# Input norm of block 0 on ScalarE, meta transposes between block 1's; expert counts and gate transposes from expert 0 to expert 2

## The reference

```
h = layer_norm(concat(meta, x))                 # 272 rows x 1024, "input norm"
mix = hybrid_mixer(h)                           # h @ w_in (1024 x 3096), conv, two chunked scans, @ w_out
h = layer_norm(alpha*h + mix)
ff = moe_ffn(h)                                 # 32 experts, top 4 per token, clamped SwiGLU
out = layer_norm(alpha*h + ff)[:, 16:]
# per expert: hid = swiglu(xb @ w_gate + b_gate, xb @ w_up + b_up); yb = hid @ w_down + b_down
# each of w_gate, w_up, w_down is 1024 x 1024 in float32, 4 MB; 32 experts make 403 MB
```

## Time and profile before

| what | value |
|---|---|
| median of 3 runs | 1059.69 us (1058.49 to 1059.8) |
| the profiled execution's own time | 1057.99 us |
| its span in the trace | 1056.2 us |
| PE, PEld busy | 1019.8 us (97%), 448.6 us (42%) |
| DVE, ACT, POOL busy | 228.7 us, 143.8 us, 30.6 us |
| read from memory | 424.59 MB, 403 GB/s over the span |

### The profile page before, as it was taken

The page is one execution under the profiler, slowest core; times in us unless marked ns, Lnnn a source line. Parts: engine busy times, 40 slices in busy tenths (PEclk is TensorE's granted clock), DMA queues, the critical chain, the costliest instruction groups (busy, mean ns, idle before and its releaser), DMA issues.

```text
span 1056.2 us, 12142 instructions
## 1 busy us (share of the span) xinstructions
PE 1019.8 (97%) x5116; PEld 448.6 (42%) x5116; DVE 228.7 (22%) x495; ACT 143.8 (14%) x348; POOL 30.6 (3%) x50
## 2 busy tenths in 40 slices
PE   8999999999999999999999999999999999999997
PEld 7888764333333333332333333333333333233332
DVE  5453652111111111111111112211111111111112
ACT  3312331111111111101110011111111111011102
POOL 1230100000000000000000000000000000000000
PEclk9999999999999999999999999999999999999999
DMA  9894889999999999999999999999999999999995
GB/s 314 274 412 191 267 314 357 432 426 436 431 429 430 433 432 431 431 434 432 431 431 434 431 429 430 431 433 430 431 428 434 432 432 429 434 426 426 428 419 238
DMA packets 40587, 426.21 MB, mean 404 GB/s; under 512 B 6986, under 2 KB 19411, under 8 KB 24036
## 3 DMA queue, kind: packets, MB, share of 16 engines
q1 hardware_dynamic: 38516, 424.12, 95.9%
q10 hardware_dynamic: 2032, 1.53, 0.6%
HBM read 424.59 MB, written 1.05 MB: 403 GB/s over the span
## 4 chain that ended last, share of the span: by engine, by line
PE 69%; DMA 29%; ACT 1%; DVE 0%; issue 0%; SPq 0%; POOL 0%; DVEq 0%; POOLq 0%; ACTq 0%
PE bank L1215 29%; DMA ring<-in_moe_w_up 18%; PE bank L1266 15%; DMA ring<-in_moe_w_gate 11%; PE bank L1195 4%; PE bank L1187 4%; PE bank L871 3%; PE bank L886 2%; PE bank L1061 2%; PE bank L1049 1%; PE bank L1003 1%; PE bank L1257 1%; PE bank L1135 1%; PE bank L964 1%; PE bank L1069 1%; PE bank L1235 1%
## 5 line engine op out<-in xcount | busy, mean ns | idle before, releaser
L1215 PE MATMUL bank<-ring,arena 128*64 128x512 f32 x1980 | 444.5, 601 | 24.5 <-DMA ring<-in_moe_w_up 20.7
L1215 PEld LDWEIGHTS bank<-ring,arena 128*64 128x64 f32 x1980 | 141.3, 138 | 297.3 <-issue 253.6
L1266 PE MATMUL bank<-ring,arena 128*64 128x512 f32 x1024 | 226.8, 595 | 1.5 <-issue 1.5
L1266 PEld LDWEIGHTS bank<-ring,arena 128*64 128x64 f32 x1024 | 71.5, 137 | 151.7 <-issue 150.1
L1663 DVE COPY arena<-bank 128x512 f32<-128x512 f32 x32 | 22.1, 692 | 326.1 <-PE bank L1266 326.1
L756 ACT ACTIVATE arena<-arena 128x512 f32<-128x512 f32 x32 | 20.1, 630 | 451.4 <-DVE arena L1650 451.4
L1195 PE MATMUL bank<-arena 64*128 64x512 f32 x256 | 72.0, 640 | 0.9 <-DVE arena L1663 0.9
L1187 PEld LDWEIGHTS bank<-arena 128*128 128x128 f32 x480 | 58.8, 196 | 22.8 <-issue 22.8
L1657 DVE TENSOR_SCALAR arena<-bank 128x512 f32<-128x512 f32 x32 | 22.1, 692 | 209.2 <-PE bank L1215 209.2
L767 ACT ACTIVATE arena<-bank 128x512 f32<-128x512 f32 x32 | 19.1, 597 | 336.3 <-PE bank L1257 336.3
L1187 PE MATMUL bank<-arena 128*128 128x128 f32 x480 | 64.5, 288 | 0.0
(11 more groups left out here) (281 smaller groups left out, 514.6 us busy)
## 6 DMA issues: line engine op xcount, KB each, us to landing
ring<-in_moe_w_down SPq DMA_DIRECT2D x25, 4096.0 KB, 28.3
ring<-in_moe_w_gate SPq DMA_DIRECT2D x24, 4096.0 KB, 24.7
ring<-in_moe_w_up SPq DMA_DIRECT2D x24, 4096.0 KB, 27.5
ring<-in_moe_w_down SPq DMA_DIRECT2D x10, 2048.0 KB, 16.6
ring<-in_moe_w_gate SPq DMA_DIRECT2D x9, 2048.0 KB, 21.4
ring<-in_moe_w_up SPq DMA_DIRECT2D x9, 2048.0 KB, 15.1
ring<-in_w_in SPq DMA_DIRECT2D x12, 1024.0 KB, 11.9
ring<-in_moe_w_gate SPq DMA_DIRECT2D x8, 1024.0 KB, 17.9
```

The costliest lines, as they stand in the source:

```text
L1215: ins = mm(b[h * SL:(h + 1) * SL, :], (xA[pp], xB)[q][:, k, par * SL:(par + 1) * SL], columns(unit_at(m, kt), h), start=False, stop=kt == ...
L1266: ins = mm(bank[6][h * SL:(h + 1) * SL, :], hidT[:, kt % 4, (kt // 4) * SL:(kt // 4 + 1) * SL], unit_at(2, kt)[:, h * 512:(h + 1) * 512], ...
```

## The change

Opening: POOL takes block 0's root first, multiplies it with the negated mean (new on DVE: `vnew`), and only then does the meta rows and block 1. ACT normalises block 0 (bias and scale), then the meta rows. DVE normalises block 1 alone, in two halves of 512 columns, each signalled. PE turns the parameters first, then block 0, then for each `kt` a piece of block 1 and one of meta. Experts: `counts`, `gate_transposes`, the list on DVE (`overfull`) and the copy on ACT are done in expert 2 instead of expert 0.

```
+TABLES = 2
@@ gpsimd
             pool.wait_ge(zeroed, 1)
+            pool.wait_ge(consts, 3)
+            pool.wait_ge(var_in, 1)
+            link(root(rstd[:, 0:1], vtmp[:, 0:1], P))
+            nc.gpsimd.tensor_tensor(vnew[:, 0:1], vnew[:, 0:1], rstd[:, 0:1], ALU.mult).then_inc(rstd_in, 1)
             pool.wait_ge(ssq, 1)
...
-            for t in range(NT):
-                pool.wait_ge(var_in, t + 1)
-                root(rstd[:, t:t + 1], vtmp[:, t:t + 1], P).then_inc(rstd_in, 1)
+            pool.wait_ge(var_in, 2)
+            root(rstd[:, 1:2], vtmp[:, 1:2], P).then_inc(rstd_in, 1)
@@ scalar
             nc.scalar.activation(meta_scr, metah, ACT.Square, bias=nmean[m0, 0:1], accum_out=mss[m0, :]).then_inc(ssq, 1)
+            act.wait_ge(rstd_in, 1)
+            nc.scalar.activation(xh[:, 0, :], xh[:, 0, :], ACT.Identity, bias=vnew[:, 0:1], scale=rstd[:, 0:1]).then_inc(hat_0, 1)
             act.wait_ge(nmean_ok, 1)
...
-                if first:
+                if isinstance(n, int) and n == TABLES:
                     act.wait_ge(GT_ps, 1)
@@ tensor
             pe.wait_ge(pads, 1)
-            pe.wait_ge(hat_m, 1)
-            for kt in range(KT - 1):
-                meta_tr(kt)
+            pe.wait_ge(params_in, 96)
+            tr(bank[3][:, 0:72], prow[:, :], ident[0:72, 0:72]).then_inc(pcol_ps, 1)
             pe.wait_ge(hat_0, 1)
             for kt in range(KT - 1):
                 x_tr(0, kt)
-            pe.wait_ge(params_in, 96)
-            tr(bank[3][:, 0:72], prow[:, :], ident[0:72, 0:72]).then_inc(pcol_ps, 1)
-            pe.wait_ge(hat_1, 1)
             for kt in range(KT - 1):
-                x_tr(1, kt).then_inc(hT_ps, 1)
+                if kt % 4 == 0:
+                    pe.wait_ge(hat_1, kt // 4 + 1)
+                x_tr(1, kt)
+                if kt == 0:
+                    pe.wait_ge(hat_m, 1)
+                meta_tr(kt).then_inc(hT_ps, 1)
             pe.wait_ge(pcol_ok, 1)
-            meta_tr(KT - 1)
             x_tr(0, KT - 1)
-            x_tr(1, KT - 1).then_inc(hT_ps, 1)
+            x_tr(1, KT - 1)
+            meta_tr(KT - 1).then_inc(hT_ps, 1)
...
                 hidden(0, bank[4], hidT_ok, g_ps)
-                if first:
+                tables = isinstance(n, int) and n == TABLES
+                if tables:
                     counts()
                     gate_transposes()
-                else:
+                if not first:
                     pe.wait_ge(yd_ok, n)
...
-                if first:
+                if tables:
                     pe.wait_ge(list_ok, 1)
@@ vector
                 link(nc.vector.bn_aggr(mv[0:n, t, :], stats[0:n, 0:2, :]))
+                if t == 0:
+                    ts(vnew[:, 0:1], mv[:, 0, 0:1], -1.0, None, ALU.mult)
                 ts(vtmp[0:n, t:t + 1], mv[0:n, t, 1:2], LN_EPS, None, ALU.add).then_inc(var_in, 1)
...
-            for t in range(NT):
-                dve.wait_ge(rstd_in, t + 1)
-                ts(xh[:, t, :], xh[:, t, :], mv[:, t, 0:1], rstd[:, t:t + 1], ALU.subtract, ALU.mult).then_inc((hat_0, hat_1)[t], 1)
+            dve.wait_ge(rstd_in, 2)
+            for h in range(2):
+                at = slice(h * 512, (h + 1) * 512)
+                ts(xh[:, 1, at], xh[:, 1, at], mv[:, 1, 0:1], rstd[:, 1:2], ALU.subtract, ALU.mult).then_inc(hat_1, 1)
...
+            def overfull():
                 dve.wait_ge(count_ps, 1)
...
                 if after is not None:
                     weigh(None if first else n, after, 1 - par)
+                if isinstance(n, int) and n == TABLES:
+                    overfull()
                 dve.wait_ge(g_ps, n + 1)
```

More of the change, by code:

```diff
@@ L824, in meta_tr @@
             def meta_tr(kt):
-                tr(hT_bank(kt)[:, 0:META], metah[:, kt * P:(kt + 1) * P], ident[0:META, 0:META])
+                return tr(hT_bank(kt)[:, 0:META], metah[:, kt * P:(kt + 1) * P], ident[0:META, 0:META])
             def x_tr(t, kt):
@@ L1634, in _ @@
             weigh(None, 0, 0)
[L1636 to L1642, removed]
+            def overfull():
+                dve.wait_ge(count_ps, 1)
+                for j in range(1, NJ):
+                    ins = ts(flag[:, j - 1, :], bank[5][0:1, 0:NE], float(SL * j), None, ALU.is_gt)
+                link(ins)
+                flagf = flag[:, :, :].rearrange("p j e -> p (j e)")
+                link(nc.vector.tensor_tensor_scan(rank, flagf, ones[0:1, 0:3 * NE], 0.0, ALU.add, ALU.mult))
+                copy(xcount, rank[:, 3 * NE - 1:3 * NE]).then_inc(list_ok, 1)
             def tile(n, par, first, after, pair):
```

## The result

The changed kernel takes **1199.52 us** (median of 5 runs, 1195.12 to 1200.46) against 1059.63 us before (5 runs): a ratio of 1.132, interval [1.130, 1.133], 140 us slower. The forecast was 1059.1 us, range 1057.1 to 1061.4. The profiled execution took 1200.46 us, with a span of 1198.7.

What follows compares the result with a forecast made beforehand. PE was taken to bound the kernel before about 157 us, the dense DMA weight stream from 182.3 us on. The opening's -0.07 and the tables' -0.5 took 1059.69 to 1059.1 us, range 1057.1 to 1061.4.

Steps and rivals of the forecast that it cites:

- Part 2: Moving counts, gate transposes and list from expert 0 to expert 2: 0.86 us leaves expert 0, -0.5 us at the end.
- The three regions: PE shifts before 157 us reach the end fully; 163 to 182 only within 3% idle DMA time; after 182 none.
- Part 1, engines: Opening: PE's block 0 pieces from 9.05 us, meta from 10.33, block 1's second half at 10.18, hidden; parameters no wait.
- Part 1, the pair: Opening: a block 1 and a meta transpose take 0.20 us together, so the projection starts 0.07 us earlier, at 12.03.
- Part 2, the size: Gate to up in expert 0 falls from 1.57 to 0.71 us; gain at the end -0.5 us, bounds 0 and -0.86.
- The rule on transfer sizes: 356 GB/s at 158 to 182 us comes from 0.5 to 1 MB pieces; starved queues, the other reading, would favour -0.86.
- The clock rival: PE drops to its lower clock in the opening or mixer: 1.7 us per stretch, two giving 1062.6 us; chance 0.04.
- The signs of being wrong: Stream rate after 182 us differs, projection starts before 11.3 or after 12.7 us, or clock falls before 148 us.
- No effect: Rival: pairs at 0.25 us or the halves' overhead eat the opening's gain, stream dense after 158: 1059.7 us; chance 0.20.
- slow pairs: Rival: slow pairs and crowded engines cost +0.53 us in the opening, tables bring nothing: 1060.2 us; chance 0.12.

Runs made afterwards that it cites:

- e2: The changed kernel with counts, gate transposes and list back in expert 0, so the new opening alone: 1059.99 us against 1058.92 for the kernel before.
- e1: The changed kernel with the table of chosen experts (maskb) in memory of its own: 1059.43 us against 1058.92 for the kernel before.
- e6: e2 with transposes in batches instead of pairs (block 0, block 1, then meta): 1058.23 us against 1058.45 for the kernel before.
- e3: The kernel before with counts, gate transposes and list in expert 2 and maskb in memory of its own: 1058.23 us against 1058.92.
- e9: The kernel before with counts, gate transposes and list in expert 1, maskb where it was: 1058.50 us against 1058.55.
- e10: The changed kernel with block 0, block 1 and meta transposed in batches and maskb in memory of its own: 1058.49 us against 1058.55 for the kernel before.
- e5: The kernel before with only PE's opening order changed: block 0, then block 1 and meta pieces in turn: 1060.10 us against 1058.45.
- e11: The kernel before with block 0's and block 1's pieces in turn after meta (equal heights, one bank): 1058.53 us, one run.
- e12: e5 with each meta piece one column tile behind, so neighbours never write one bank: 1060.00 us, one run.

## Why the prediction was wrong

**The step that failed** is the last sentence on what bounds the kernel: the end is set "by its bytes, which the change leaves alone". The change added 37.75 MB, as three passes at the end, outside the dense stream, 41.4 us each, and 13.5 us for the list. Part 2 priced four matmuls, a wait and a DVE chain, and asked for each who is late next; it did not ask whether what they read is still there two experts later. The overlap stood in two lines of the kernel, both outside the diff. The trace of before had the list's length as well, in 32 passes and no issue from the list's loop: a branch not taken, whose condition the moved instructions compute. No rival held a change of it.

**Point by point.**
- *The three regions*: the first held: the 1.5 us of e2's opening reached SP at 157 us in full, and the end within its interval. So did the third: 429 to 430 GB/s from 182.3 to 1036 us in e1 to e6, as in the earlier trace rows, and the 0.86 us that came back in expert 2 cost nothing to be seen (e3). The second, between 163 and 182 us, is not resolved.
- *Part 1, engines*: held. Block 0's pieces at 9.09 (forecast 9.05), the first meta piece at 10.32 (10.33), parameters no wait. Block 1's second half came later than forecast, at 10.46 instead of 10.18, and was still hidden. Block 0's root, beside DVE's statistics, took 0.56 us, not 0.907.
- *Part 1, the pair*: mis-sized. I took 0.20 between 0.18 and 0.30; it was 0.42, above the upper bound. The row with 0.16 from a meta piece to a block piece was there; I averaged over it with two intervals between equal heights, and the way back, 0.26, had no clean row. The term was +1.36 (e2) in place of -0.07, and what reached the end +1.1. The projection's start was also the wrong mark for a gain: e6 starts 0.2 us earlier and has lost it by 23.58 us.
- *Part 2, the size*: gate to up as forecast to the hundredth. -0.5 forecast; e3's medians give -0.7, between the bounds 0 and -0.86, but its interval, 0.9993 [0.9984, 1.0002], reaches past both bounds, and e9 and e10 are 1.0 within theirs. The size is not resolved.
- *The rule on transfer sizes* (the Trainium skill, DMA: Bandwidth & Descriptors, Bandwidth) would leave no more than the idle share to be had, some 0.7 us. The page's figures are for transfers issued from GpSimd, and here SP issues them. e3's interval holds that and 0.86 alike, so no run here tells the two readings apart.
- *The clock rival*: in kind it came true in the profiled execution of the changed kernel. Its second group of the projection starts at 26.68 against 25.14 in e2, 1.54 us for a stretch that the prediction priced at 1.7. e1 and e2, with the same opening, stand at 1.00 there. A longer wait does not tell them apart: before block 0's pieces PE waited 0.58 us in the changed kernel and 0.75 in e2, which kept its clock. Why it fell in that execution stays open, and these runs do not tie it to the change.
- *The signs of being wrong*: two of those that the prediction named were there, a projection after 12.7 us (13.94) and a lower clock before 148 us. Neither points at the passes, which are nearly all of the loss.
- *No effect, slow pairs*: without the overwritten mask the change is e1, 1.0007 [0.9998, 1.0016], which is what the rival of slow pairs with 1060.2 us came nearest to. e1's 1059.43 us is also within 0.4 us of the forecast 1059.1. That would have been luck: the opening lost some 1.5 us at SP where a small gain was forecast, and the tables gave part of it back.

**The sum as measured**: opening +1.1, tables -0.7 to 0, passes and list 137.7, together 138 to 139, of 139.9. The remaining 1 to 2 us lie within the spread of the changed kernel's runs (1195.1 to 1200.5), which is wider than before; its passes run at granted clocks of 0.88 to 0.91, and 32 matmuls of the third pass took 9.88 us against 7.11 in the first. Left open: which expert was listed, and whether one was listed three times for its three limits or three once each; the trace shows only three passes.

## What to carry to other kernels

Before moving work later, list what it reads, and for each operand who next writes that memory; with hand-placed buffers the answer is in address arithmetic, not in the diff, and no semaphore protects a lifetime that nobody moved. Count first when a result is far off: instructions, passes and bytes named the cause here before any duration was looked at. Where moved instructions compute a branch's condition, price the branch taken as a rival.

## What the runs showed of the hardware that I had not expected

Transposes of 16-row and 128-row pieces in turn cost 0.16 and 0.26 us, 0.42 a pair, against 0.06 and 0.12 in batches of one height; same bank or other bank, and the readiness of the data, made no difference (e5, e11, e12). A piece of 72 rows between two of 128 showed no such cost (e5). Grouping the 16-row pieces was worth 1.6 us in the new opening (e2 to e6); its new division of work gained nothing that lasted to the projection's second group.
